# Linear attention's chunk means: the squares of a head's two halves are added on VectorE, and one mean product per chunk stands in place of two

## The chip, the cores and the metric

The kernel is one launch on one core of a Trainium2 chip. The metric is the device time of the launch in microseconds (us); before the change it is 3007.17 us, the median of three runs (3007.15, 3007.17 and 3008.69). Five engines run their own instruction queues side by side and meet only at semaphores: PE (TensorE, matmuls), DVE (VectorE), ACT (ScalarE), POOL (GpSimd) and SP (SyncE, which issues the DMAs).

## The reference

The program is two transformer-like blocks over 512 tokens of width 1024. The change lies in the gated linear attention of the last layer. Its output is normalised per token and head over the 256 values of the head, and then gated:

```python
def _rmsnorm(x, gain):
    xf = x.astype(jnp.float32)
    y = xf * lax.rsqrt(jnp.mean(xf * xf, axis=-1, keepdims=True) + RMS_EPS)
    return (y * gain.astype(jnp.float32)).astype(x.dtype)

# in _gla_mixer: 4 heads (GLA_HEADS) of 256 values (GLA_HV)
    _, o = lax.scan(step, state0, (qc, kc, vc, gc))
    o = o.transpose(1, 0, 3, 2, 4).reshape(bsz, seq, GLA_HEADS, GLA_HV).astype(h.dtype)
    gate = jax.nn.silu(g_out).reshape(bsz, seq, GLA_HEADS, GLA_HV)
    o = _rmsnorm(o, norm_gain) * gate
    return o.reshape(bsz, seq, GLA_VAL_DIM) @ w_out
```

The mean of squares over a head's 256 values is what is computed in another way after the change.

## The kernel before

Activations lie transposed: features on the 128 partitions, tokens along the free dimension. A head's 256 values are therefore two halves of 128 partitions. The recurrence goes over the 512 tokens in four chunks of 128 (`NCH = 4`, `CH = 128`). All order is written out by hand, each engine's queue as a Python function, with counting semaphores between them.

PE's queue for chunk c is: `local(c)` (the part inside the chunk, 8 matmuls of 128 columns, L1528), `chunk_mean(c - 1)` (L1537), `carry(c)` (what the state gains, 4 matmuls of 256 columns, L1544), `across(c)` (the part from the state, L1553, which signals `lo_done`). After chunk 3 come the output products: `glo_half(o, half)` multiplies 256 tokens of the normalised result with output tile o in 24 matmuls of 256 columns (L893, L894, L895). Their order is `glo_half(2, 0)`, `chunk_mean(3)`, `glo_half(3, 0)`, then `glo_half(0, 0)` and `glo_half(1, 0)`, then the second halves of tokens.

`chunk_mean(c)` multiplies a 128x128 matrix that holds 1/256 with the squares. There are 8 square slices of 128 tokens per chunk (4 heads, 2 halves). Two matmuls of 512 columns go into one PSUM bank: the first with all first halves, the second with all second halves, accumulated.

ACT's queue for chunk c: squares of 128x1024 into `lsq` (L2070, signals `lo_sq`), a copy of the raw result into `loT` (L2071, signals `lo_copied`), and the square root of the mean (L2077, signals `lo_std`). Between them stand `high_piece(0)` and `high_piece(1)` (L1609), the high parts of the finished chunks 0 and 1. `high_piece(1)` stands in front of the root of chunk 2.

POOL multiplies each copied chunk by the gate in place (L883, 128x1024, signals `lo_gated`).

DVE's queue: `state_step(c)` (L2764, 4 instructions, PSUM and SBUF), `inverse(c)` (L2787, a reciprocal of 128x512), `scaled(c)` (L2774, the product with the inverse root) and `low_piece(i)` (L2781, the low parts). `glo_half(o, 0)` needs `low_piece(0)` and `low_piece(1)`; the second halves of tokens need the later pieces one after the other. Of the pieces, 0 is chunk 0, 1 is chunk 1, 2 and 3 are halves of chunk 2, and 4 to 7 quarters of chunk 3.

Of the kernel before, what the change touches and what calls it, by code (L numbers as in the profile page):

```python
# [32 lines left out]
ALU = mybir.AluOpType  # L33
# [3 lines left out]
T = 512  # L37
# [36 lines left out]
CH = P  # L74
# [89 lines left out]
M_ID, M_D, M_256, M_128, M_64, M_ROT = range(6)  # L164
# [102 lines left out]
def program(nc, a, out, gates):  # L267

    with ExitStack() as ctx:
        sems = {}  # L270

        def S(name):
            if name not in sems:
                sems[name] = ctx.enter_context(nc.semaphore(name))
            return sems[name]
# [33 lines left out]
        pb = ctx.enter_context(nc.psum_tensor("pb", [P, 8, 512], F32))  # L309
# [17 lines left out]
        def mat(n):  # L327
            return mats[:, n, :]
# [164 lines left out]
        at_lev = G.at  # L493
# [12 lines left out]
        la = Area(at_lev + 4 * T).take(4, T)  # L506
        loT = Area(at_lev + 8 * T).take(DC, T)
        lsq = Area(at_lev + 6 * T).take(DC, CH)
        lkt = Area(at_gw).take(TT, GH, P)

        pieces = [(0, 0, 8), (1, 0, 8), (2, 0, 4), (2, 4, 8), (3, 0, 2), (3, 2, 4), (3, 4, 6), (3, 6, 8)]
# [376 lines left out]
        def _(pe):  # L888
            mm = pe.matmul
# [59 lines left out]
            for c in range(DC):  # L949
# [3 lines left out]
                if c == 4:  # L953
                    slot(T_QKD)
                pe.wait_ge(S("h_done"), c + 1)
                m = three(pb[:, QK_BANK[0], :], rhigh[:, w, c, :], rlow[:, w, c, :], hS[:, 0, c, :], hS[:, 1, c, :],
                          c == 0, c == DC - 1)
# [176 lines left out]
            for o in range(DC):  # L1134
# [7 lines left out]
                for c in range(6):  # L1142
                    if o == 0:
                        pe.wait_ge(S("cat_split"), c + 1)
                    m = three(pb[:, b0 + 2 + c // 4, :], rhigh[:, w, c, :], rlow[:, w, c, :], cat_high[:, c, :],
                              cat_low[:, c, :], c % 4 == 0, c in (3, 5))
# [7 lines left out]
            for i in range(PH + 1):  # L1154
# [9 lines left out]
                if i >= 1:  # L1164
# [6 lines left out]
                    for half in range(2):  # L1171
                        for t in range(TT):
                            m = mm(pb[:, 2 + 2 * (s % 2) + half, t * P:(t + 1) * P],  # L1173
                                   qh[:, s % 2, half, t * P:(t + 1) * P], keys[:, half, :],
                                   start=True, stop=True)
# [31 lines left out]
            for n in range(3):  # L1207
                for t in range(TT):
                    src = (choice[:, n, t, :] if n < 2 else
                           score[:, t, :, :].rearrange("p h k -> p (h k)"))  # L1210
                    m = pe.transpose(pb[:, 4 + n, t * P:(t + 1) * P], src, mat(M_ID))
# [60 lines left out]
            for half in range(2):  # L1272
                w = slot(T_PLE + 5 * half)
                for o in range(4):
                    if half:
                        pe.wait_ge(S("x_upd"), X_PEER + o + 1)
                    for c in range(2):
                        m = mm(pb[:, o, :], ring[:, w, o * 2 + c, :], pT[:, c, :], start=c == 0, stop=c == 1)  # L1278
# [192 lines left out]
            for c in range(DC):  # L1471
                m = three(pb[0:16, 4, :], gkwh[:, c, :], gkwl[:, c, :], hS[:, 0, c, :], hS[:, 1, c, :],
                          c == 0, c == DC - 1)
            m.then_inc(S("gk_low"), 1)
            for n in range(4 * TT):
# [4 lines left out]
                if n == 0:  # L1480
                    pe.wait_ge(S("gk_low"), 2)
                    pe.wait_ge(S("l_copied"), 8)
                    for h in range(GH):
                        m = mm(pb[:, h, :], gku[0:16, h * P:(h + 1) * P], gkl[0:16, :], start=True, stop=True)
# [6 lines left out]
            for t in range(TT):  # L1491
                for h in range(GH):
                    m = pe.transpose(pb[:, t, h * P:(h + 1) * P], lks[:, 0, h * T + t * P:h * T + (t + 1) * P],
                                     mat(M_ID))
# [3 lines left out]
            for n in range(NL + 1):  # L1498
# [9 lines left out]
                for t in range(TT):  # L1508
                    for h in range(GH):
# [5 lines left out]
                        m = mm(pb[:, t, h * P:(h + 1) * P], k, q, start=True, stop=True)  # L1515
# [14 lines left out]

            def chunk_mean(c):

                pe.wait_ge(S("lo_sq"), c + 1)
                if c >= 2:
                    pe.wait_ge(S("lo_std"), c - 1)
                for v in range(2):
                    m = mm(pb[:, 4 + c % 2, :].rearrange("p (h i) -> p h i", i=CH), mat(M_256),  # L1537
                           lsq.rearrange("p (h v) i -> p v h i", v=2)[:, v, :, :], start=v == 0, stop=v == 1)
                m.then_inc(S("lo_mean"), 1)

            def carry(c):

# [549 lines left out]
        def _(ve):  # L2092
# [663 lines left out]
            def state_step(c):  # L2756

                ve.wait_ge(S("state_mm"), c + 1)
                ve.wait_ge(S("state_done"), c + 1)
                if c >= 1:  # L2760

                    ve.wait_ge(S("lo_done"), c)
                for h in range(GH):
                    m = ve.scalar_tensor_tensor(state[(c + 1) % 2][:, h, :], state[c % 2][:, h, :], ebl[:, h * NCH + c:h * NCH + c + 1],  # L2764
                                                pb[:, (2 if c else 4) + h // 2, (h % 2) * 256:(h % 2 + 1) * 256],
                                                ALU.mult, ALU.add)
                m.then_inc(S("state_done"), 1)
# [8 lines left out]
            def low_piece(i):  # L2776

                c, n0, n1 = pieces[i]
                at = slice(c * CH, (c + 1) * CH)
                ve.wait_ge(S("h_high"), H_LO + i + 1)  # L2780
                ve.tensor_tensor(hS[:, 1, n0:n1, at], loT[:, n0:n1, at], hS[:, 0, n0:n1, at].bitcast(F32),  # L2781
                                 ALU.subtract).then_inc(S("h_done"), 1)

            def inverse(c):

                ve.wait_ge(S("lo_std"), c + 1)
                ve.reciprocal(rstd[:, c % 2, :], rstd[:, c % 2, :]).then_inc(S("rstd_done"), 1)  # L2787

            def scaled(c):

                ve.wait_ge(S("rstd_done"), 6 + c + 1)
                ve.wait_ge(S("lo_gated"), c + 1)
                for i in range(8):
                    if pieces[i][0] == c:
                        scale_piece(i).then_inc(S("h_raw"), 1)
                ve.sem_inc(S("lo_scaled"), 1)

            state_step(0)
            inverse(0)
            state_step(1)  # L2800
            scaled(0)
            inverse(1)
            state_step(2)
            scaled(1)
            low_piece(0)
            low_piece(1)
            inverse(2)
            scaled(2)
# [119 lines left out]
```

## Time and profile before

| what | value |
|---|---|
| median of three runs | 3007.17 us |
| the profiled execution's own time | 3008.21 us |
| its span, first to last instruction | 3006.4 us |
| PE busy | 2977.3 us, 99% |
| DVE busy | 1694.8 us, 56% |
| ACT busy | 1275.5 us, 42% |
| POOL busy | 1428.6 us, 48% |
| mean granted TensorE clock | 0.997 |

The trace is of one execution. Its own time is 1.8 us above its span and 1.04 us above the median. A timeline row gives the start from the span's beginning, the length, the engine, the line in the kernel, the operation with output and inputs, and in brackets the idle time before it and what ended it. PE's rows overlap, since matmuls are pipelined; the pace of a group is read from one start to the next. An fp32 matmul of the program leaves two matmul records. DVE's and ACT's rows start up to 0.1 us before the instruction in front of them ends. `s_arena` is the SBUF area that holds most intermediate tiles, `lsq`, `loT` and the new `lsum` among them; `pb` is PSUM.

### The profile page before, as it was taken

How to read it: one execution, taken by the hardware profiler on the slowest of the kernel's cores; microseconds unless marked ns; L12 is line 12 of the kernel's file. 1: busy time of each engine (PE TensorE's matmuls, PEld its weight loads, DVE VectorE, ACT ScalarE, POOL GpSimd, SP SyncE). 2: the span in 40 equal slices, each digit the busy share in tenths (PEclk: the TensorE clock that was granted, in tenths of full speed). 3: DMA queues.
4: the chain of work that ended last, by engine and by line, in shares of the span. 5: the costliest groups of instructions: out<-in, count | busy, mean ns of one | idle time of the engine just before them, and what ended most of it. 6: DMA issues, size and time to landing. Idle time of an engine off the chain costs nothing.

```text
span 3006.4 us, 40609 instructions
## 1 busy us (share of the span) xinstructions
PE 2977.3 (99%) x15170; PEld 2561.0 (85%) x15170; DVE 1694.8 (56%) x2918; ACT 1275.5 (42%) x2109; POOL 1428.6 (48%) x747
## 2 busy tenths in 40 slices
PE   9999999999999999999999999999999999999998
PEld 7887888888888888899999997778888889888887
DVE  5826359998999601168888875363122436641223
ACT  6555344325777633333333334354233334542332
POOL 6732444444334444577777603644444433344442
PEclk9999999999999999999999999999999999999999
DMA  4242332444687865599999953212333322123332
GB/s 147 92 139 79 105 101 85 137 146 133 177 214 200 214 192 165 189 341 375 364 368 366 368 188 112 81 61 98 98 95 94 110 70 71 49 92 98 98 98 84
DMA packets 331164, 473.18 MB, mean 157 GB/s; under 512 B 125765, under 2 KB 235237, under 8 KB 330489
## 3 DMA queue, kind: packets, MB, share of 16 engines
q1 hardware_dynamic: 308472, 403.79, 42.4%
q0 software_dynamic: 22528, 67.19, 6.1%
q8 instruction: 106, 1.74, 0.2%
q14 instruction: 58, 0.47, 0.0%
HBM read 405.97 MB, written 60.86 MB: 155 GB/s over the span
## 4 chain that ended last, share of the span: by engine, by line
PE 95%; issue 1%; DVE 1%; POOL 1%; DMA 1%; ACT 0%; SPq 0%; DVEq 0%; POOLq 0%; ACTq 0%
PE pb L893 29%; PE pb L895 29%; PE pb L894 29%; PE pb L1223 2%; PE pb L1515 1%; POOL s_over L753 1%; PE pb L1074 1%; PE pb L1102 0%; PE pb L1173 0%; PE pb L1356 0%; DMA s_ring<-w 0%; PE pb L1376 0%; PE pb L1041 0%; PE pb L1278 0%; PE pb L1365 0%
## 5 line engine op out<-in xcount | busy, mean ns | idle before, releaser
L753 POOL TENSOR_TENSOR s_over<-s_ring,s_rhigh 128x1024 fp32r<-128x1024 f32 x401 | 986.8, 2463 | 1375.3 <-ACT s_rhigh L1623 1374.7
L1623 ACT ACTIVATE s_rhigh<-s_ring 128x1024 fp32r<-128x1024 f32 x525 | 555.8, 1060 | 1098.3 <-DMA s_ring<-w 496.7
L893 PE MATMUL pb<-s_over,s_rhigh 128*128 128x512 f32 (+1 forms) x2392 | 876.5, 366 | 0.5 <-DVE s_over L2470 0.4
L895 PE MATMUL pb<-s_over,s_over 128*128 128x512 f32 (+1 forms) x2392 | 872.8, 365 | 0.0
L894 PE MATMUL pb<-s_over,s_rhigh 128*128 128x512 f32 (+1 forms) x2392 | 872.7, 365 | 0.0
L893 PE MATMUL pb<-s_hS,s_rhigh 128*128 128x512 f32 (+1 forms) x1664 | 650.3, 391 | 5.0 <-DVE s_hS L2781 2.5
L895 PE MATMUL pb<-s_hS,s_over 128*128 128x512 f32 (+1 forms) x1672 | 645.3, 386 | 0.0
L894 PE MATMUL pb<-s_hS,s_rhigh 128*128 128x512 f32 (+1 forms) x1664 | 642.2, 386 | 0.0
L893 PEld LDWEIGHTS pb<-s_over,s_rhigh 128*128 128x128 f32 x2392 | 449.1, 188 | 55.1 <-issue 1.0
L894 PEld LDWEIGHTS pb<-s_over,s_rhigh 128*128 128x128 f32 x2392 | 449.1, 188 | 53.4 <-issue 1.0
L895 PEld LDWEIGHTS pb<-s_over,s_over 128*128 128x128 f32 x2392 | 449.0, 188 | 52.8
L893 PEld LDWEIGHTS pb<-s_hS,s_rhigh 128*128 128x128 f32 x1664 | 313.3, 188 | 71.9 <-issue 6.8
L895 PEld LDWEIGHTS pb<-s_hS,s_over 128*128 128x128 f32 x1672 | 314.0, 188 | 64.8
L894 PEld LDWEIGHTS pb<-s_hS,s_rhigh 128*128 128x128 f32 x1664 | 313.4, 188 | 63.7 <-issue 3.8
L2310 DVE TENSOR_TENSOR s_xT<-pb,s_xT 128x512 f32<-128x512 f32 x95 | 65.5, 690 | 305.2 <-PE pb L895 305.2
L2470 DVE TENSOR_TENSOR s_over<-s_ring,s_rhigh 128x1024 fp32r<-128x1024 f32 x124 | 151.9, 1225 | 93.3 <-ACT s_rhigh L1623 93.0
L2449 DVE TENSOR_SCALAR s_over<-s_arena,s_over 128x128 fp32r<-128x128 f32 x384 | 202.1, 595 | 0.0
L816 POOL DMA_INDIRECT s_arena<-acts,s_arena x128 | 163.2, 1275 | 38.9 <-issue 38.7
L2464 DVE TENSOR_TENSOR s_over<-s_std,s_over 128x384 fp32r<-128x384 f32 x128 | 77.6, 607 | 132.7 <-ACT s_over L1801 132.7
L2659 DVE SCALAR_TENSOR_TENSOR s_arena<-pb,s_rstd 128x512 f32<-128x512 f32 x64 | 44.0, 691 | 178.5 <-PE pb L895 178.4
L2478 DVE TENSOR_TENSOR s_std<-s_arena 128x384 f32<-128x384 f32 x128 | 74.7, 584 | 100.2 <-DMA s_arena<-gates 99.0
L1819 ACT ACTIVATE s_over<-s_over,s_arena 128x128 fp32r<-128x128 f32 x384 | 117.9, 395 | 7.2 <-DVE s_over L2449 6.9
(310 smaller groups left out, 3160.1 us busy)
## 6 DMA issues: line engine op xcount, KB each, us to landing
s_ring<-w SPq DMA_DIRECT2D x272, 512.0 KB, 3.5
s_ring<-eu SPq DMA_DIRECT2D x128, 512.0 KB, 4.0
s_ring<-ev SPq DMA_DIRECT2D x128, 512.0 KB, 6.1
acts<-s_arena SPq DMA_DIRECT2D x128, 256.0 KB, 4.1
s_arena<-acts SPq DMA_DIRECT2D x128, 192.0 KB, 5.1
s_arena<-gates SPq DMA_DIRECT2D x128, 192.0 KB, 6.3
gates<-s_arena SPq DMA_DIRECT2D x36, 512.0 KB, 5.6
gates<-s_arena SPq DMA_DIRECT2D x6, 1024.0 KB, 7.5
```

The source lines that it names most:

```text
L753: gp.tensor_tensor(rlow[:, s, :, :], ring[:, s, :, :], rhigh[:, s, :, :].bitcast(F32), ALU.subtract).then_inc(S("w_split"), 1)
L816: gp.indirect_dma_start(s_act[:, j:j + 1], None, acts1, bass.IndirectOffsetOnAxis(ap=s_el[:, j:j + 1], axis=0))\
L893: mm(dst, a_high, b_high, start=start, stop=False)
L894: mm(dst, a_high, b_low, start=False, stop=False)
L895: return mm(dst, a_low, b_high, start=False, stop=stop)
L1623: sc.activation(rhigh[:, s, :, :], ring[:, s, :, :], ACT.Copy).then_inc(S("w_high"), 1)
L1819: sc.activation(oh1[:, t % 16, 1, :], oh1[:, t % 16, 0, :].bitcast(F32), ACT.Identity, scale=g_ratio[:, t:t + 1]).then_inc(S("oh_low"), 1)
L2310: return ve.tensor_tensor(xT[:, c, :], pb[:, bank, :], xT[:, c, :], ALU.add)\
L2449: ve.tensor_scalar(oh1[:, t % 16, 0, :], iota, chT[:, 0, t:t + 1], g_high[:, t:t + 1].bitcast(F32), ALU.is_equal, ALU.mult).then_inc(S("oh ...
L2464: ve.tensor_tensor(actE[:, k % NA, 1, :], std[:, k % 2, 0:TD], actE[:, k % NA, 0, :].bitcast(F32), ALU.subtract).then_inc(S("e_act"), 1)
L2470: ve.tensor_tensor(rlow[:, n % RING, :, :], ring[:, n % RING, :, :], rhigh[:, n % RING, :, :].bitcast(F32), ALU.subtract).then_inc(S("w_sp ...
L2478: ve.tensor_tensor(std[:, e % 2, 0:TD], va_in[:, e % 4, 0:TD], gtile[:, e % 4, 0:TD], ALU.mult)\
```

## The change

ACT still writes the 8 square slices. A new DVE instruction per chunk, `sum_halves(c)`, adds the second halves to the first into `lsum` (128x512) and signals `lo_sum`. `chunk_mean(c)` is one matmul of 512 columns on `lsum` and waits for `lo_sum` in place of `lo_sq`. `lsum` is a single buffer, so `sum_halves(c)` also waits for the mean of the chunk before.

```diff
+        lsum = Area(at_lev + 5 * T).take(T)
...
             def chunk_mean(c):
 
-                pe.wait_ge(S("lo_sq"), c + 1)
+                pe.wait_ge(S("lo_sum"), c + 1)
                 if c >= 2:
                     pe.wait_ge(S("lo_std"), c - 1)
-                for v in range(2):
-                    m = mm(pb[:, 4 + c % 2, :].rearrange("p (h i) -> p h i", i=CH), mat(M_256),
-                           lsq.rearrange("p (h v) i -> p v h i", v=2)[:, v, :, :], start=v == 0, stop=v == 1)
-                m.then_inc(S("lo_mean"), 1)
+                mm(pb[:, 4 + c % 2, :], mat(M_256), lsum, start=True, stop=True).then_inc(S("lo_mean"), 1)
...
+            def sum_halves(c):
+
+                ve.wait_ge(S("lo_sq"), c + 1)
+                if c >= 1:
+                    ve.wait_ge(S("lo_mean"), c)
+                v = lsq.rearrange("p (h v) i -> p v h i", v=2)
+                ve.tensor_tensor(lsum.rearrange("p (h i) -> p h i", i=CH), v[:, 0, :, :], v[:, 1, :, :], ALU.add)\
+                    .then_inc(S("lo_sum"), 1)
...
             state_step(0)
+            sum_halves(0)
             inverse(0)
             state_step(1)
+            sum_halves(1)
             scaled(0)
             inverse(1)
             state_step(2)
+            sum_halves(2)
             scaled(1)
             low_piece(0)
+            sum_halves(3)
             low_piece(1)
```

On DVE, from `state_step(0)` to `inverse(2)`, the queue stood as follows before (s_std and s_sq hold the state by turns, L2787 is the reciprocal, L2774 `scaled`, L2781 the two `low_piece`):

```order
L2764 SCALAR_TENSOR_TENSOR s_std<-s_sq,s_arena,pb 128x256 x3
L2787 RECIPROCAL s_rstd<-s_rstd 128x512 [waits lo_std]
L2764 SCALAR_TENSOR_TENSOR s_sq<-s_std,s_arena,pb 128x256 [waits lo_done,state_done,state_mm]
L2764 SCALAR_TENSOR_TENSOR s_sq<-s_std,s_arena,pb 128x256 x3
L2774 TENSOR_TENSOR s_arena<-s_arena,s_rstd 128x8x128 [waits lo_gated,rstd_done]
L2787 RECIPROCAL s_rstd<-s_rstd 128x512 [waits lo_std]
L2764 SCALAR_TENSOR_TENSOR s_std<-s_sq,s_arena,pb 128x256 [waits lo_done,state_done,state_mm]
L2764 SCALAR_TENSOR_TENSOR s_std<-s_sq,s_arena,pb 128x256 x3
L2774 TENSOR_TENSOR s_arena<-s_arena,s_rstd 128x8x128 [waits lo_gated,rstd_done]
L2781 TENSOR_TENSOR s_hS<-s_arena,s_hS 128x8x128 [waits h_high] x2
L2787 RECIPROCAL s_rstd<-s_rstd 128x512 [waits lo_std]
```

The same stretch after the change reads so; L2788 is `sum_halves`, and the other lines have moved a little (L2762 for L2764, L2794 for L2787, L2772 for L2774, L2779 for L2781):

```order
L2788 TENSOR_TENSOR s_arena<-s_arena 128x512 [waits lo_sq]
L2794 RECIPROCAL s_rstd<-s_rstd 128x512 [waits lo_std]
L2762 SCALAR_TENSOR_TENSOR s_sq<-s_std,s_arena,pb 128x256 [waits lo_done,state_done,state_mm]
L2762 SCALAR_TENSOR_TENSOR s_sq<-s_std,s_arena,pb 128x256 x3
L2788 TENSOR_TENSOR s_arena<-s_arena 128x512 [waits lo_mean,lo_sq]
L2772 TENSOR_TENSOR s_arena<-s_arena,s_rstd 128x8x128 [waits lo_gated,rstd_done]
L2794 RECIPROCAL s_rstd<-s_rstd 128x512 [waits lo_std]
L2762 SCALAR_TENSOR_TENSOR s_std<-s_sq,s_arena,pb 128x256 [waits lo_done,state_done,state_mm]
L2762 SCALAR_TENSOR_TENSOR s_std<-s_sq,s_arena,pb 128x256 x3
L2788 TENSOR_TENSOR s_arena<-s_arena 128x512 [waits lo_mean,lo_sq]
L2772 TENSOR_TENSOR s_arena<-s_arena,s_rstd 128x8x128 [waits lo_gated,rstd_done]
L2779 TENSOR_TENSOR s_hS<-s_arena,s_hS 128x8x128 [waits h_high]
```

Behind the last of these rows the fourth sum stands between `low_piece(0)` and `low_piece(1)`. The sums of chunks 1 and 2 stand behind a `state_step` and ahead of a `scaled`.

On PE, at the mean of chunk 1 (between `local(2)` and `carry(2)`), the queue was before:

```order
L1528 MATMUL pb<-s_arena 128x128 [waits lo_copied]
L1528 MATMUL pb<-s_arena 128x128 x7
L1537 MATMUL pb<-s_arena,s_mats 128x512 [waits lo_sq]
L1537 MATMUL pb<-s_arena,s_mats 128x512
L1544 MATMUL pb<-s_arena 128x256 [waits state_done]
```

And it is after the change:

```order
L1529 MATMUL pb<-s_arena 128x128 [waits lo_copied]
L1529 MATMUL pb<-s_arena 128x128 x7
L1537 MATMUL pb<-s_arena,s_mats 128x512 [waits lo_sum]
L1542 MATMUL pb<-s_arena 128x256 [waits state_done]
L1542 MATMUL pb<-s_arena 128x256 x3
```

One matmul is gone and the other waits for DVE's sum. Nothing else on PE, and nothing on ACT, POOL or SP, is added, removed or moved.

## Rows read from the trace of the kernel before

**Rows 1.** The page: the span, and each engine's busy time.
```profile
span 3006.4 us, 40609 instructions
PE 2977.3 (99%) x15170; PEld 2561.0 (85%) x15170; DVE 1694.8 (56%) x2918; ACT 1275.5 (42%) x2109; POOL 1428.6 (48%) x747
```

**Rows 2.** Timeline of PE: start, length, engine, line, operands, count, idle before.
```profile
2575.73 1.95 PE L1537 MATMUL pb<-s_arena,s_mats 128*128 128x512 f32 x4
2577.52 1.89 PE L1544 MATMUL pb<-s_arena 128*128 128x256 f32 x8
2579.25 1.95 PE L1553 MATMUL pb<-s_arena,s_std 128*128 128x128 f32 x16
...
2582.82 1.88 PE L1537 MATMUL pb<-s_arena,s_mats 128*128 128x512 f32 x4
2584.54 1.89 PE L1544 MATMUL pb<-s_arena 128*128 128x256 f32 x8
...
2589.83 1.88 PE L1537 MATMUL pb<-s_arena,s_mats 128*128 128x512 f32 x4
2591.55 1.95 PE L1553 MATMUL pb<-s_arena,s_std 128*128 128x128 f32 x16
2596.00 0.36 PE L893 MATMUL pb<-s_hS,s_rhigh 128*128 128x256 f32 x1 [2.50 <-DVE s_hS L2781]
...
2600.14 2.22 PE L1537 MATMUL pb<-s_arena,s_mats 128*128 128x512 f32 x4
```

**Rows 3.** Timeline of DVE, the same columns.
```profile
2578.52 3.35 DVE L2787 RECIPROCAL s_rstd<-s_rstd 128x512 f32<-128x512 f32 x1 [6.85 <-ACT s_rstd L2077]
2581.79 1.56 DVE L2764 SCALAR_TENSOR_TENSOR s_sq<-s_std,s_arena,pb 128x256 f32<-128x256 f32 x4
2583.26 1.22 DVE L2774 TENSOR_TENSOR s_arena<-s_arena,s_rstd 128x1024 f32<-128x1024 f32 x1
2585.46 3.35 DVE L2787 RECIPROCAL s_rstd<-s_rstd 128x512 f32<-128x512 f32 x1 [0.98 <-ACT s_rstd L2077]
...
2590.20 1.22 DVE L2774 TENSOR_TENSOR s_arena<-s_arena,s_rstd 128x1024 f32<-128x1024 f32 x1
2591.34 3.38 DVE L2781 TENSOR_TENSOR s_hS<-s_arena,s_hS 128x1024 fp32r<-128x1024 f32 x1
```

**Rows 4.** The chain that ended last, in order of time: two of its pieces.
```profile
2583.25 3.46 POOL s_arena L883
...
2594.64 1.22 DVE s_hS L2781
```

**Rows 5.** Timeline of ACT.
```profile
2574.58 1.00 ACT L2070 ACTIVATE s_arena<-pb 128x1024 f32<-128x1024 f32 x1
...
2576.51 1.28 ACT L2077 ACT_TABLE_LOAD   x1
2577.80 0.69 ACT L2077 ACTIVATE s_rstd<-pb,s_small 128x512 f32<-128x512 f32 x1
2581.23 1.02 ACT L2070 ACTIVATE s_arena<-pb 128x1024 f32<-128x1024 f32 x1 [2.74 <-PE pb L1553]
2582.15 1.02 ACT L2071 ACTIVATE s_arena<-pb 128x1024 f32<-128x1024 f32 x1
2584.74 0.69 ACT L2077 ACTIVATE s_rstd<-pb,s_small 128x512 f32<-128x512 f32 x1 [1.57 <-PE pb L1537]
```

**Rows 6.** Timeline of POOL.
```profile
2576.63 2.34 POOL L883 TENSOR_TENSOR s_arena<-s_arena 128x1024 f32<-128x1024 f32 x1 [1.96 <-ACT s_arena L2071]
...
2590.26 3.37 POOL L883 TENSOR_TENSOR s_arena<-s_arena 128x1024 f32<-128x1024 f32 x1 [3.56 <-ACT s_arena L2071]
```

**Rows 7.** L2110's instructions (ns min/median/max), then one with POOL's beside it.
```profile
L2110 DVE TENSOR_TENSOR s_rstd<-s_rstd,s_sq x48: 676/681/2907, 393.0 to 2989.4; 128x512 f32<-128x512 f32 x48
2624.38 2.91 DVE L2110 TENSOR_TENSOR s_rstd<-s_rstd,s_sq 128x512 f32<-128x512 f32 x1
2624.34 2.40 POOL L753 TENSOR_TENSOR s_over<-s_ring,s_rhigh 128x1024 fp32r<-128x1024 f32 x1 [0.43 <-ACT s_rhigh L1623]
```

**Rows 8.** One stretch: us, busy of PE, PEld, DVE, ACT, POOL, PEclk, DMA.
```profile
2597.40:2600.80 3.40, 3.40 (x16) 3.07 (x15) 3.01 (x3) 0.00 (x0) 0.70 (x1) 0.50 0.02 5
```

## The prediction, written before the result was known

> **What bounds the kernel now.** I read the page first: PE is busy for 2977.3 us of a span of 3006.4 [rows 1]. So the time is PE's, and a change pays only if it takes work off PE without making PE wait. The page is an average, and the change touches about 30 us, so I went to PE's timeline there. PE is without a gap from the first chunk mean to the end of the recurrence, and then stands idle 2.50 us ahead of the first output product at 2596.00, released by DVE's low parts, L2781 [rows 2]. Behind 2596.00 it has no wait that concerns this change. So the span moves by two things: when the output products start (call it T1, now 2596.00), and what is taken off PE behind T1.
>
> DVE's timeline says what makes T1. `scaled(1)` runs 2590.20 to 2591.42. `low_piece(0)` takes 3.38 us from 2591.34 [rows 3], though its twin `low_piece(1)` takes 1.22 us in the chain of waits, 2594.64 to 2595.86 [rows 4]. Beside the slow one, POOL's gate product runs 2590.26 to 2593.63, 3.37 us, where the first of its kind took 2.34 with DVE idle [rows 6]. So POOL waited for `scaled(1)`, then took its turn, and `low_piece(0)` waited for all of it: 2.2 us. A DVE instruction with two SBUF inputs and a POOL product exclude each other for whole instructions. A second place says so with the width of the new sum: 48 additions of 128x512 take 0.68 us at best and 2.91 at worst, and the 2.91 one starts at 2624.38, 0.04 us behind a POOL product [rows 7]. The ends fit: 2624.34 + 2.40 + 0.55 = 2627.29.
>
> **What the change removes.** One of two mean matmuls in each of four chunks. Two take 2577.52 - 2575.73 = 1.79 us in chunk 0, 2584.54 - 2582.82 = 1.72 in chunk 1, and 2591.55 - 2589.83 = 1.72 in chunk 2 [rows 2]. One is worth 0.86 us, the four 3.4 us. Only the fourth lies behind T1; the other three shorten a stretch that ends in a wait.
>
> **What it adds.** Four DVE additions of 128x512, both inputs in SBUF. The trace has no such addition on these tiles. From below each costs 0.68, the best of the 48, and from above 2.91, one that meets POOL [rows 7]. Which it is follows from the schedule, chunk by chunk. All times are from the span's start.
>
> Chunk 0. The squares end at 2574.58 + 1.00 = 2575.58 [rows 5]; DVE is idle until 2578.52 [rows 3]. The sum ends at 2576.3, the mean starts near 2576.4 in place of 2575.73, and `carry(1)` at 2576.4 + 0.86 = 2577.26 in place of 2577.52: 0.26 gained. The first root does not move, since it waits for a table load until 2577.79 [rows 5]; so neither does the first reciprocal, nor `state_step(1)` behind it, 2581.79 to 2583.35 [rows 3].
>
> Chunk 1. All of PE is 0.26 earlier, so the squares start at 2580.97 (before: 2581.23), the copy ends at 2582.15 + 1.02 - 0.26 = 2582.91 [rows 5], and POOL's second product starts at 2583.25 - 0.26 = 2582.99 [rows 4]. But the sum stands behind `state_step(1)`, whose place the row at 2583.26 now holds [rows 3]. It comes 0.27 us behind POOL, so it is blocked until 2582.99 + 2.34 = 2585.33 and ends at 2585.95. `chunk_mean(1)` starts at 2586.05 in place of 2582.82. After its saving `carry(2)` starts at 2586.91 against 2584.54 [rows 2]: 2.37 late. This is the step that I hold to be decisive.
>
> The next chunk follows. The root of chunk 1 started 2584.74 - 2582.82 = 1.92 behind the mean's start [rows 2, 5]; with one matmul less that is 1.06: 2587.11 to 2587.80. The reciprocal (3.35) ends at 2591.18 and `state_step(2)` (1.56) at 2592.65 [rows 3]. On PE `carry(2)` (1.73) and `across(2)` (its 1.95 from 2579.25 end at 2581.20, just ahead of the squares at 2581.23) make the third squares start at 2586.91 + 1.73 + 1.98 = 2590.62, and the copy end at 2592.57 [rows 2, 5].
>
> Chunk 2. The sum can start at 2592.6 and POOL's third product at 2592.65. That is a tie. If DVE is first, the sum ends at 2593.25, POOL holds until 2595.5, and `scaled(1)` ends at 2596.6. If POOL is first, the sum ends at 2595.6 and `scaled(1)` at 2596.75. Both give `scaled(1)` within 0.2 us, against 2591.42 before.
>
> Chunk 3. The fourth sum stands ahead of `low_piece(1)`, and needs the fourth squares. ACT does them only after `high_piece(1)` (2596.65 to 2597.7, it needs `scaled(1)`), and the root of chunk 2 (to 2598.3). They run 2598.2 to 2599.2. The sum ends at 2599.9, `low_piece(1)` at 2601.1, and T1 is 2601.25. In the other order of chunk 2 the fourth `across` ends later, the squares at 2599.5, and T1 is 2601.5. I take 2601.3.
>
> **The sum.** T1 moves by 2601.3 - 2596.0 = +5.3. Behind T1 the fourth mean loses 0.86, and it never waits, as its sum is done before T1. Behind it nothing new is late: the second halves of tokens hang on the fourth mean by root and reciprocal as before, and PE has the same three half products, 72 matmuls, in between. That makes +4.4.
>
> The clock is the last term. PE's idle 2.50 us were followed by half clock (0.50, 1.2 GHz) from 2597.40 to 2600.80 [rows 8]: 3.4 us in which half the work was done, a loss of 1.7. After the change the pause ahead of T1 is about 5 us, and there is a new one of some 3.3 us ahead of `chunk_mean(1)`. Half clock after the longer pause may partly fall into the pause itself, which gives back up to 1.7. Half clock after the new pause slows `carry(2)` and `across(2)` by up to 1.7, and their lateness only partly reaches T1. I take -0.3 for both, with -1.4 to +1.2 kept for the range: +4.1 in all.
>
> The profiled execution took 3008.21, so its like would take 3012.3. It stands 1.04 above the median; on the median of 3007.17 the forecast is 3011.3.
>
> **A rule weighed.** The rows show a DVE product recorded at 2583.26, with its full speed of 1.22 us, beside a POOL product recorded at 2583.25 that took 3.46 [rows 3, 4]. The Trainium skill (SBUF — State Buffer, section "Who interferes with whom") says that a DVE instruction with two SBUF inputs and a GpSimd instruction that reads SBUF use one locked port pair, that the one issued first keeps it for the whole instruction, and that issue order decides who blocks. The trace agrees that it is a lock and no sharing. By the record starts alone the rule would have POOL block DVE at 2583.25, and the row shows the reverse, so leads under about 0.03 us cannot be read off. By the rule chunk 1 costs the full block (lead 0.27 us) and the sum is +4.1; if the two only slowed each other a little it would be the +2.7 of the second rival.
>
> **The rivals.**
> - The loss turns out larger, by a second lock. `low_piece(1)` follows the fourth sum at 2599.9; POOL's fourth product starts when the copy behind the fourth squares ends, near 2600.2. The margin is 0.3 us. If the sum runs late, because `low_piece(0)` is still busy when the squares end, POOL is waiting when the sum ends, as it was in front of `low_piece(0)` before. It then holds `low_piece(1)` until 2600.2 + 2.34, and T1 is near 2603.8. That is +7.8 - 0.86 = +6.9, 3014.1 us: slower by over 0.2%. For it: the tie of chunk 2 and half clock both shift this meeting. Against: the copy takes 1 us and the sum 0.68, so in the ordinary case DVE wins. It decides where `low_piece(0)` ends later than the fourth squares.
> - The second sum wins the lock or POOL comes later than I think. Then it ends at 2583.95, the mean starts at 2584.05, and `carry(2)` at 2584.92, 0.38 late. The squares of chunk 2 start at 2588.63; POOL's third product runs 2590.65 to 2593.0, the third sum is held by it to 2593.6, `scaled(1)` ends at 2594.75, the fourth squares (behind `high_piece(1)` and the root) at 2597.6, `low_piece(1)` at 2599.45. T1 is 2599.6, +3.6 - 0.86 = +2.7: 3009.9. Against it speaks the lead of 0.27.
> - The sums are covered, as in chunk 0, and T1 stays where DVE and POOL put it before. Then only the fourth mean's 0.86 us is gained: 3006.3. The fourth sum ahead of `low_piece(1)` speaks against it even without any block, since its squares wait behind two ACT instructions. All 3.4 us would be 3003.8, which the wait ahead of T1 excludes for three quarters of it.
> - The change does not do what it says: excluded by the order shown, one matmul less and one addition more per chunk.
>
> **How the numbers follow.** Forecast 0.60, its own range 3009.9 to 3012.5. The second lock 0.17, the second sum first 0.17, covered 0.06. About 0.2% (6 us) is what a measurement of this kernel can tell from no change. Forecast and second sum first lie within it; the second lock lies just beyond, as does a forecast with the worst clock: slower 0.20, within 0.78, faster 0.02. The range reaches from below the third case to the second lock: 3008.8 to 3014.3.
>
> **What would show it.** In the profile after: the second sum near 2583.3 taking 2.6 us beside a POOL product, and PE idle some 3.3 us ahead of the second mean; `low_piece(1)` directly behind the fourth sum near 2601; PE idle some 5 us ahead of the output products; the fourth mean one matmul, without a wait. I would be wrong if the second sum takes 0.7 us, if T1 is earlier than 2599, or if half clock appears more than twice from 2570 on.

## The result, and the profile after

The changed kernel takes 3011.6 us (median of 20 runs, 3008.59 to 3014.44) against 3007.13 us (median of 20, 3004.46 to 3009.44). The ratio is 1.0015, 95% interval 1.0009 to 1.0021: 4.5 us slower, 0.15%. The forecast was 3011.3. The profiled execution of after has a span of 3010.5 us against 3006.4. The experiments ran on other chips. On the first of these (e1 to e4) most executions, those of before included, took about 24 us longer (median of before 3031.53, fastest 3005.06); the traces there show pauses of PE and 20 to 27 us of half clock near 1300 us, far ahead of the change. So ratios and traces are compared there, not medians.

Two lengths are used from here on. L is the time from the first product of `local(0)` to the first output product, R that to the first addition to x_T, the running activations, behind them (DVE, L2310; L2308 after). Before, L is 2596.00 - 2570.19 = 25.81 and R 43.72. PE's timeline of after (start, length, line, count, idle before):

```profile
2570.70 2.05 PE L1529 MATMUL pb<-s_arena 128*128 128x128 f32 x16 [1.02 <-DVE s_arena L2719]
...
2576.97 1.10 PE L1537 MATMUL pb<-s_arena,s_mats 128*128 128x512 f32 x2 [0.65 <-DVE s_arena L2788]
2577.90 1.89 PE L1542 MATMUL pb<-s_arena 128*128 128x256 f32 x8
...
2586.57 1.12 PE L1537 MATMUL pb<-s_arena,s_mats 128*128 128x512 f32 x2 [3.21 <-DVE s_arena L2788]
2587.53 3.21 PE L1542 MATMUL pb<-s_arena 128*128 128x256 f32 x8
2590.54 2.34 PE L1551 MATMUL pb<-s_arena,s_sq 128*128 128x128 f32 x16
...
2594.72 1.12 PE L1537 MATMUL pb<-s_arena,s_mats 128*128 128x512 f32 x2
...
2600.98 0.36 PE L894 MATMUL pb<-s_hS,s_rhigh 128*128 128x256 f32 x1 [3.36 <-DVE s_hS L2779]
...
2605.42 1.02 PE L1537 MATMUL pb<-s_arena,s_mats 128*128 128x512 f32 x2
```

The recurrence begins 0.51 us later than before, for reasons ahead of the change. L is 2600.98 - 2570.70 = 30.28, 4.47 longer. Against the gapless PE of before [rows 2] there are three pauses: 0.65 ahead of the first mean, 3.21 ahead of the second, 3.36 ahead of the output products (2.50 before). `carry(2)` took 1.72 us before and takes 3.01 here.

DVE's timeline of after, from the first state step with a sum behind it:

```profile
2582.30 1.56 DVE L2762 SCALAR_TENSOR_TENSOR s_sq<-s_std,s_arena,pb 128x256 f32<-128x256 f32 x4
2583.78 2.73 DVE L2788 TENSOR_TENSOR s_arena<-s_arena 128x512 f32<-128x512 f32 x1
2586.43 1.21 DVE L2772 TENSOR_TENSOR s_arena<-s_arena,s_rstd 128x1024 f32<-128x1024 f32 x1
2588.45 3.35 DVE L2794 RECIPROCAL s_rstd<-s_rstd 128x512 f32<-128x512 f32 x1 [0.80 <-ACT s_rstd L2075]
...
2593.97 0.69 DVE L2788 TENSOR_TENSOR s_arena<-s_arena 128x512 f32<-128x512 f32 x1 [0.69 <-ACT s_arena L2068]
2594.58 1.22 DVE L2772 TENSOR_TENSOR s_arena<-s_arena,s_rstd 128x1024 f32<-128x1024 f32 x1
2595.71 3.39 DVE L2779 TENSOR_TENSOR s_hS<-s_arena,s_hS 128x1024 fp32r<-128x1024 f32 x1
2599.02 0.68 DVE L2788 TENSOR_TENSOR s_arena<-s_arena 128x512 f32<-128x512 f32 x1
2599.62 1.21 DVE L2779 TENSOR_TENSOR s_hS<-s_arena,s_hS 128x1024 fp32r<-128x1024 f32 x1
```

And POOL's gate products of chunks 1, 2 and 3 in the same execution:

```profile
2583.62 2.34 POOL L884 TENSOR_TENSOR s_arena<-s_arena 128x1024 f32<-128x1024 f32 x1 [4.14 <-ACT s_arena L2069]
2594.93 3.09 POOL L884 TENSOR_TENSOR s_arena<-s_arena 128x1024 f32<-128x1024 f32 x1 [8.96 <-ACT s_arena L2069]
2599.68 3.39 POOL L884 TENSOR_TENSOR s_arena<-s_arena 128x1024 f32<-128x1024 f32 x1 [1.66 <-ACT s_arena L2069]
```

The second sum is recorded at 2583.78, 0.16 behind POOL's start, and takes 2.73 in place of 0.7: the step on which the prediction rested. In the row of before at this place POOL was recorded 0.01 ahead, and `scaled(0)` went first [rows 3, 4]. Here POOL leads by enough. By the Trainium skill (SBUF — State Buffer, "Who interferes with whom") the one that issues first keeps the port pair for its whole instruction, and the trace agrees: POOL's product has its full 2.34, and the sum ends 0.55 behind it. Further down the meeting of before is repeated: `low_piece(0)` takes 3.39. The last meeting is near: `low_piece(1)` at 2599.62, POOL at 2599.68, and DVE goes first.

The clock, in two stretches of after (us, busy of PE, PEld, DVE, ACT, POOL, granted clock, DMA share, GB/s):

```profile
2587.90:2591.30 3.40, 3.40 (x12) 2.80 (x11) 2.85 (x1) 1.46 (x2) 0.00 (x0) 0.51 0.00 0
2601.60:2605.00 3.40, 3.40 (x18) 3.40 (x18) 3.37 (x3) 0.00 (x0) 1.47 (x1) 0.50 0.02 5
```

There are two stretches of half clock (1.2 GHz), one behind each long pause, where before had one [rows 8].

### The profile page after: what moved, and what is told of

It reads as the page before. It is cut to its first block, busy times and chain, and to the rows that moved or that the text cites. A ratio compares the mean times of both kernels' runs of the same rounds, so it can differ in the third digit from the quotient of the medians.

```text
span 3010.5 us, 40600 instructions
## 1 busy us (share of the span) xinstructions
PE 2976.5 (99%) x15162; PEld 2561.4 (85%) x15162; DVE 1693.8 (56%) x2922; ACT 1275.6 (42%) x2109; POOL 1423.8 (47%) x747
## 3 DMA queue, kind: packets, MB, share of 16 engines
q1 hardware_dynamic: 308472, 403.79, 42.3%
## 4 chain that ended last, share of the span: by engine, by line
PE 94%; issue 2%; DVE 1%; ACT 1%; POOL 1%; DMA 1%; SPq 0%; DVEq 0%; POOLq 0%; ACTq 0%
PE pb L894 29%; PE pb L895 29%; PE pb L896 29%; PE pb L1224 2%; PE pb L1516 1%; POOL s_over L754 1%; PE pb L1075 1%; PE pb L1103 0%; PE pb L1174 0%; PE pb L1357 0%; DMA s_ring<-w 0%; PE pb L1377 0%; ACT s_rhigh L1621 0%; PE pb L1042 0%; PE pb L1279 0%
## 5 line engine op out<-in xcount | busy, mean ns | idle before, releaser
L2308 DVE TENSOR_TENSOR s_xT<-pb,s_xT 128x512 f32<-128x512 f32 x95 | 65.5, 690 | 305.2 <-PE pb L896 305.1
```

The lines of the kernel that those rows point to most:

```text
L2308: return ve.tensor_tensor(xT[:, c, :], pb[:, bank, :], xT[:, c, :], ALU.add)\
```

## The experiments

One table first. "Half" is the time of half clock while PE worked inside R, read off the granted clock; the last column but one takes half of it off R.

| kernel | L | R | half | R - half/2 | ratio to before, 95% |
|---|---|---|---|---|---|
| before | 25.81 | 43.72 | 3.4 | 42.0 | |
| after | 30.28 | 47.29 | 6.8 | 43.9 | 1.0015, 1.0009 to 1.0021 |
| e1 second sum free of POOL | 29.00 | 47.11 | 5.8 | 44.2 | 1.0014, 0.9996 to 1.0032 |
| e2 fourth sum behind | 29.68 | 46.69 | 6.8 | 43.3 | 0.9990, 0.9966 to 1.0014 |
| e3 one mean matmul, no sums | 24.98 | 41.99 | 3.4 | 40.3 | 1.0003, 0.9973 to 1.0033 |
| e4 sums unread | 28.70 | 47.09 | 4.6 | 44.8 | 1.0027, 1.0012 to 1.0042 |
| e5 after, first POOL waits | 29.21 | 44.71 | 0 | 44.7 | 1.0014, 1.0005 to 1.0023 |
| e6 before, POOL waits | 23.72 | 40.10 | 0 | 40.1 | 0.9991, 0.9982 to 1.0000 |
| e7 both | 25.35 | 42.25 | 0 | 42.3 | 0.9999, 0.9990 to 1.0008 |
| e8 chunks 0 and 3 only | 25.86 | 41.37 | 0 | 41.4 | 1.0000, 0.9990 to 1.0009 |
| e9 before, pause filled | 25.81 | 42.19 | 0 | 42.2 | 0.9997, 0.9988 to 1.0006 |
| e10 after, pauses filled | 31.07 | 48.07 | 3.4 | 46.4 | 1.0009, 1.0000 to 1.0018 |
| e11 after, POOL out of the way | 27.17 | 45.40 | 6.1 | 42.4 | 1.0004, 0.9994 to 1.0013 |
| e12 best | 23.59 | 39.11 | 0 | 39.1 | 0.9989, 0.9980 to 0.9998 |

Each row's L and R are of one profiled execution, and a stretch of half clock moves R by about 1.5, so the medians and the traces are read side by side. Outside R the profiled executions of before, after and e5 to e12 differ too, by up to 3.9 us (span minus R, 2960.4 in e11 to 2964.3 in e10). The intervals of e1 to e4 are 0.3 to 0.6% wide, and only e4's excludes no change; there the traces decide.

**e1. The second sum freed of POOL.**

```diff
                 gp.wait_ge(S("lo_copied"), c + 1)
+                if c == 1:
+                    gp.wait_ge(S("lo_sum"), 2)
```

> The changed kernel, with one wait more: POOL's gate product of chunk 1 starts only when the second sum is done, so POOL cannot hold the port there. L is the time from the first product of local(0) to the first output product: 25.81 us before (2570.19 to 2596.00), 30.28 after (2570.70 to 2600.98). Theory (the second sum is blocked by POOL): its length falls from 2.73 to 0.69 us, PE's idle time ahead of the second mean from 3.21 to about 1.2 us, no half clock follows it, and L is near 29.4, the figure of the prediction's second rival. Rival (the wait comes from the place in DVE's queue behind state_step(1) alone): the second sum and the idle time stay as they are, L 30.3.

DVE's timeline of e1 and the product of chunk 1 on POOL:

```profile
2607.70 0.68 DVE L2790 TENSOR_TENSOR s_arena<-s_arena 128x512 f32<-128x512 f32 x1
...
2615.07 0.68 DVE L2790 TENSOR_TENSOR s_arena<-s_arena 128x512 f32<-128x512 f32 x1
2615.67 3.37 DVE L2774 TENSOR_TENSOR s_arena<-s_arena,s_rstd 128x1024 f32<-128x1024 f32 x1
```
```profile
2608.53 3.21 POOL L886 TENSOR_TENSOR s_arena<-s_arena 128x1024 f32<-128x1024 f32 x1 [5.12 <-DVE s_arena L2790]
```

The second sum takes 0.68, PE's pause ahead of the second mean falls from 3.21 to 1.16, and L is 29.00: the mechanism is shown. But 2 us of pause gave only 1.3 us of L, and R hardly moved: the lock now catches `scaled(1)` (3.37, the order "DVE first" of the forecast's chunk 2), the pause ahead of the output products grows to 4.91, and half clock follows it.

**e2. The fourth sum behind `low_piece(1)`.** In DVE's queue `sum_halves(3)` and `low_piece(1)` change places.

> The changed kernel with the fourth sum behind low_piece(1) in DVE's queue. After the change the fourth squares were done at 2598.68, ahead of low_piece(0)'s end at 2599.10, so the sum cost only itself. Theory: L falls by 0.6 us to 29.7, and the fourth mean still waits for nothing, since a half output product of 3 to 4 us stands in front of it. Rival (the step as the prediction put it: the fourth sum waits for its squares behind ACT's queue and holds low_piece(1)): L falls by 2 us or more.

L is 29.68. The first theory holds: in this schedule the fourth sum costs its own 0.6 us.

**e3. One of the two mean matmuls, no sums.**

```diff
-                for v in range(2):
-                    m = mm(..., lsq...[:, v, :, :], start=v == 0, stop=v == 1)
+                m = mm(..., lsq...[:, 0, :, :], start=True, stop=True)
```

> The kernel before with only the first of the two mean matmuls of each chunk, and no sums: half of the squares are left out of the means. It is the largest gain that PE's side of the change could bring. Theory (the start of the output products is set by DVE and POOL): L stays at 25.8 within 0.3, only the fourth mean's 0.86 us is gained, about 3006.3 us beside 3007.2. Rival (the recurrence is bound by PE): L falls by 2.6 to 23.2, 3.4 us in all, 3003.8 us.

Neither. L falls by 0.83 to 24.98, and from the start of the output products to the x_T addition it is 17.01 in place of 17.91, both with 3.4 us of half clock: 0.90 more. PE's part of the change is worth 1.7 us at most (R 43.72 - 41.99), twice what the prediction's rival allowed. Of the 2.6 us saved ahead of the output products some 1.75 don't reach them: PE now waits for the state twice (0.42 and 0.79), the rest stands in no wait that the timeline lists, and the pause of 2.50 stays. The lock is still there, at other instructions: `scaled(0)` takes 2.56 and `scaled(1)` 2.18, and both low pieces have their 1.22.

**e4. The sums on DVE, read by nobody.** PE has both mean matmuls again; ACT's new wait stands ahead of the squares of chunk c, from 1 on, and `sum_halves(c)` waits for `lo_sum` in place of `lo_mean`.

```diff
             def chunk_mean(c):
-                pe.wait_ge(S("lo_sum"), c + 1)
-                mm(pb[:, 4 + c % 2, :], mat(M_256), lsum, ...)
+                pe.wait_ge(S("lo_sq"), c + 1)
+                for v in range(2):
+                    m = mm(..., lsq...[:, v, :, :], start=v == 0, stop=v == 1)
...
+                    sc.wait_ge(S("lo_sum"), c)
```

> The kernel before with the four sums at the change's places in DVE's queue, but both mean matmuls kept and PE waiting for the squares as before; nobody reads the sums (the next squares wait until the sum of the last is done). It tells DVE's load from PE's wait. Theory A (the sums' place in DVE's queue and their lock with POOL already delay the chain state_step, scaled, low_piece): L near 28.9, 3 us over before, with hardly any idle time of PE ahead of the second mean. Theory B (the cost is PE waiting for the sums): L within 0.7 us of 25.8.

DVE's timeline of e4, from the second sum on, and POOL's product beside it:

```profile
2605.98 0.68 DVE L2792 TENSOR_TENSOR s_arena<-s_arena 128x512 f32<-128x512 f32 x1
2606.58 3.38 DVE L2776 TENSOR_TENSOR s_arena<-s_arena,s_rstd 128x1024 f32<-128x1024 f32 x1
...
2619.62 0.69 DVE L2792 TENSOR_TENSOR s_arena<-s_arena 128x512 f32<-128x512 f32 x1 [1.48 <-ACT s_arena L2072]
2620.23 1.22 DVE L2783 TENSOR_TENSOR s_hS<-s_arena,s_hS 128x1024 fp32r<-128x1024 f32 x1
```
```profile
2605.96 2.91 POOL L884 TENSOR_TENSOR s_arena<-s_arena 128x1024 f32<-128x1024 f32 x1 [4.26 <-ACT s_arena L2073]
```

L is 28.70, 2.9 over before, with PE never waiting for a sum. So theory A: the sums in DVE's queue make L 2.9 longer by themselves, though `scaled(0)` is blocked here and not the sum, so this need not be the same 2.9 of the 4.47 after the change. The sum, recorded 0.02 behind POOL, goes first; POOL takes its turn behind it, and `scaled(0)` pays 2.2 us. Putting one more instruction between `state_step` and `scaled` hands POOL the port.

**e5. POOL held back, first attempt.**

```diff
+                if c == 1:
+                    gp.wait_ge(S("lo_scaled"), 1)
+                if c == 2:
+                    gp.wait_ge(S("h_done"), H_LO + 2)
```

> The changed kernel, with POOL held back so that its gate products never run beside DVE work on the path: the product of chunk 1 waits until scaled(0) is done, that of chunk 2 until low_piece(1) is done. Nothing else moves. L (first product of local(0) to first output product) was 25.81 us before and 30.28 after; with the second sum alone freed of POOL it was 29.00, with the sums unread and PE waiting for the squares 28.70. Theory (most of the loss is DVE blocked by POOL, now at one instruction and now at another, and the rest is the fourth sum waiting ahead of low_piece(1)): no DVE instruction of 0.7 or 1.2 us takes over 1.3, and L is near 27.3. Rival (the loss is the sums' own 0.7 us each and PE's wait for them): L stays over 29.

L is 29.21, and this run tests less than it was meant to. POOL's product of chunk 1 did not wait:

```profile
2581.56 2.73 DVE L2792 TENSOR_TENSOR s_arena<-s_arena 128x512 f32<-128x512 f32 x1
2584.22 1.21 DVE L2776 TENSOR_TENSOR s_arena<-s_arena,s_rstd 128x1024 f32<-128x1024 f32 x1
```
```profile
2581.41 2.34 POOL L888 TENSOR_TENSOR s_arena<-s_arena 128x1024 f32<-128x1024 f32 x1 [4.13 <-ACT s_arena L2073]
```

`lo_scaled` is raised by a count instruction of its own behind the products. POOL had passed its wait by 2581.41, while `scaled(0)` began at 2584.22. That this separate instruction ran ahead is the reading that e11 supports, where the product's own count holds POOL back; it was not measured by itself. The second wait worked.

**e11. POOL held back on the product's own count.** `h_raw` is raised by the products of `scaled` themselves.

```diff
+                if c == 1:
+                    gp.wait_ge(S("h_raw"), raw(H_LO) + 1)
+                if c == 2:
+                    gp.wait_ge(S("h_done"), H_LO + 2)
```

> The changed kernel with POOL's product of chunk 1 held back until scaled(0) has really finished, and that of chunk 2 until low_piece(1) has. In the run of this kind before, the first of these waits was passed 2.8 us ahead of scaled(0), because it hung on a count that DVE's queue raises before the product is done; here it hangs on the product's own count. Theory (POOL's lock and the fourth sum's place make the whole lateness): the second sum takes 0.7, PE's pause ahead of the second mean is 1.2, L is near 27.2. Rival: L stays over 29.

DVE's timeline of e11, around the fourth sum:

```profile
2590.08 1.22 DVE L2783 TENSOR_TENSOR s_hS<-s_arena,s_hS 128x1024 fp32r<-128x1024 f32 x1
2593.08 0.69 DVE L2792 TENSOR_TENSOR s_arena<-s_arena 128x512 f32<-128x512 f32 x1 [1.78 <-ACT s_arena L2072]
2593.69 1.22 DVE L2783 TENSOR_TENSOR s_hS<-s_arena,s_hS 128x1024 fp32r<-128x1024 f32 x1
```

L is 27.17 as expected; no DVE instruction up to `low_piece(1)` is blocked. The fourth sum stands and waits 1.78 us for its squares, with `low_piece(1)` behind it: by these rows its place costs 1.78 + 0.6 = 2.4 us here (no run moved it with POOL out of the way and nothing else), and only 0.6 in e2, where POOL held `low_piece(0)` over the same time. Two causes in parallel hide each other.

**e6. The POOL waits without the change.** The kernel before, with the edit of e5.

> The kernel before, both mean matmuls and no sums, with the same two waits on POOL. Theory (the 3.38 us of low_piece(0) was POOL's lock and set the start of the output products): low_piece(0) takes 1.2, L falls by 2.1 to 23.7, PE's pause ahead of the output products from 2.50 to about 0.4 us, and no half clock follows it, which gives up to 1.7 more: 2 to 4 us faster than before. Rival (something else starts the output products, or POOL's late products delay the second halves of the tokens): L within 0.5 of 25.8, or the gain is lost behind the start.

DVE's timeline of e6 (both low pieces in one row), and the first output product:

```profile
2588.52 1.22 DVE L2778 TENSOR_TENSOR s_arena<-s_arena,s_rstd 128x1024 f32<-128x1024 f32 x1
2589.65 2.43 DVE L2785 TENSOR_TENSOR s_hS<-s_arena,s_hS 128x1024 fp32r<-128x1024 f32 x2
```
```profile
2592.23 0.36 PE L897 MATMUL pb<-s_hS,s_rhigh 128*128 128x256 f32 x1 [0.41 <-DVE s_hS L2785]
```

L is 23.72 and the pause 0.41, as expected. The gain is 2.7 us (3003.23 against 3005.96), with an interval from 0.9982 to 1.0000 that just reaches no change. The first wait was passed early here too, as in e5; it did no harm, since `scaled(0)` keeps its 1.22. So what set the start of the output products before was POOL's lock on `low_piece(0)`. With POOL out of the way on both sides the change costs 27.17 - 23.72 = 3.45 us of L; with POOL in the way on both, 4.47. So about 1.0 of the 4.47 goes with the lock; it is the smaller part.

**e7. Both, and the sums moved.** The changed kernel with the edit of e5, `sum_halves(1)` and `(2)` ahead of their `state_step`, the fourth behind `low_piece(1)`.

> The changed kernel with the same two waits on POOL, the sums of chunks 1 and 2 ahead of their state_step, and the fourth behind low_piece(1). Theory: the second mean waits for nothing, L is near 24.0 (the state_steps are 0.7 later each), and the fourth mean saves its 0.86 behind the start; so about as fast as the kernel before with the POOL waits alone, within 1 us, and 2 to 4 us faster than before. Rival (the sums cost on this path wherever they stand): L over 26.

L is 25.35 and not 24.0; R is 2.15 over e6. PE waits five times in L, 0.63, 0.44, 0.38, 0.43 and 1.53 us, and 1.01 behind it. This run is not clean, as POOL still blocks two instructions: its product of chunk 1, again not held back, makes `scaled(0)` take 2.21 in place of 1.22, and its product of chunk 2, released by `low_piece(1)`, makes the fourth sum take 2.83, ahead of the 1.01 pause behind L. With all of that 1.0 taken off, L would be near 24.4, by estimate, still 0.6 over e6 with two middle mean matmuls fewer; what the middle sums alone cost was not measured.

**e8. Chunks 0 and 3 alone.** `chunk_mean` waits for the sum and uses one matmul for c in (0, 3), and for the squares with two matmuls otherwise; the fourth sum stands behind `low_piece(1)`.

> The change made for chunks 0 and 3 alone, with the fourth sum behind low_piece(1); chunks 1 and 2 keep two mean matmuls and PE waits for the squares there; POOL as before. Theory: the first sum is covered and the fourth stands beside the first half output product, so L is that of the kernel before, 25.6 to 25.8, and from the start of the output products to the first x_T addition (L2310, 17.91 us before) 0.9 us less: 0.9 to 1.1 us faster. Rival: the fourth sum meets POOL's last product and the fourth mean waits for it, which takes the gain back.

L is 25.86, but by another way: `carry(1)` comes 0.15 earlier, POOL's product of chunk 1 is now recorded 0.15 ahead of `scaled(0)` (2583.60 against 2583.75), and `scaled(0)` takes 3.27, `scaled(1)` 2.37, while the low pieces have their 1.22. From the first output product to the x_T addition it takes 15.51 at full clock, where e6 and e9 take 16.38: 0.87 saved. The time shows no gain (ratio 1.0000, interval 0.9990 to 1.0009); 0.9 us is below what it can show.

**e9 and e10. The pauses filled.** In e9 two matmuls that nobody reads follow `across(3)` of the kernel before; in e10, the changed kernel, three stand there and three ahead of the second mean:

```diff
+            def busy(n):
+                for _ in range(n):
+                    mm(pb[:, 5, :], mat(M_256), lqs[:, 0, 0:T], start=True, stop=True)
...
+            pe.wait_ge(S("lo_std"), 2)
+            busy(2)
             glo_half(2, 0)
```

> The kernel before, with two matmuls of 512 columns whose result nobody reads between across(3) and the first output product, in PE's pause of 2.50 us there (each 0.86 us). R is the time from the first product of local(0) to the first x_T addition, 43.72 us before, and holds 3.41 us of half clock under work. Theory (half clock follows the pause, and costs half of its length): no half clock behind the start of the output products, R near 42.0, L unchanged at 25.8, and 1 to 1.7 us faster than before. Rival (half clock comes from something else, or the pause left over is enough for it): R and the time unchanged.

> The changed kernel with three such matmuls ahead of the second mean (pause of 3.21 us) and three ahead of the first output product (3.36 us). It had 6.83 us of half clock under work, in two stretches, and R 47.29. Theory: none of the two is left, R near 43.9 to 44.5, L near 28.6 to 30.3, and the time 1.5 to 3.4 us under that of the changed kernel, so 1 to 3 us over before. Rival (the loss is waiting alone): R over 46 and the time 4 to 5 us over before.

e9: L stays at 25.81, no half clock, R 42.19 (expected 42.0), 1.53 less than before. The trace is as the theory has it, but it is one execution, and e8 and e5 have no half clock behind pauses of 2.68 and 3.21 either; so that the filled pause took it away is not shown. The time is 0.7 us lower, and the interval holds both no gain and 1.7 us.

e10 is divided. The time is as the theory has it: ratio 1.0009, 2.3 us over before where the changed kernel is 4.5 over. R is 48.07, on the rival's side, and L the longest of all. But the profiled execution is the slowest of its 11 (3014.17 us, median 3008.72). What lies outside R differs by 3.9 us at most between the traces, so the usual execution of e10 probably has a shorter R, and no trace shows it. DVE and POOL of e10:

```profile
2594.30 0.68 DVE L2797 TENSOR_TENSOR s_arena<-s_arena 128x512 f32<-128x512 f32 x1
2594.90 3.37 DVE L2781 TENSOR_TENSOR s_arena<-s_arena,s_rstd 128x1024 f32<-128x1024 f32 x1
2598.19 1.21 DVE L2788 TENSOR_TENSOR s_hS<-s_arena,s_hS 128x1024 fp32r<-128x1024 f32 x1
2600.88 0.69 DVE L2797 TENSOR_TENSOR s_arena<-s_arena 128x512 f32<-128x512 f32 x1 [1.48 <-ACT s_arena L2077]
2601.49 1.22 DVE L2788 TENSOR_TENSOR s_hS<-s_arena,s_hS 128x1024 fp32r<-128x1024 f32 x1
```
```profile
2594.36 2.83 POOL L884 TENSOR_TENSOR s_arena<-s_arena 128x1024 f32<-128x1024 f32 x1 [7.29 <-ACT s_arena L2078]
```

With no half clock inside L this execution has the prediction's schedule line by line: the tie of chunk 2 (sum 2594.30, POOL 2594.36), the sum first, `scaled(1)` blocked, the fourth sum waiting for its squares. L is 2602.86 - 2571.79 = 31.07, against the forecast 2601.3 - 2570.19 = 31.1.

**e12. A version to beat both.** e8 with

```diff
+                if c == 1:
+                    gp.wait_ge(S("h_raw"), raw(H_LO) + 1)
+                if c == 2:
+                    gp.wait_ge(S("lo_sum"), 2)
+                if c == 3:
+                    gp.wait_ge(S("h_raw"), raw(H_LO + 3) + 1)
```

> A version to beat both: the change in chunks 0 and 3 alone, fourth sum behind low_piece(1), and POOL's products of chunks 1 to 3 held back until scaled(0), the fourth sum and scaled(2) are done. Theory: L near 23.7 as with the POOL waits alone, where R was 40.10 without half clock, and the fourth mean saves its 0.86: R near 39.3, 3 to 4 us faster than before. Rival (POOL's products of chunks 2 and 3 come too late for the second halves of the tokens): a pause of PE over 0.5 us in front of them, and a time no better than with the POOL waits alone (0.9991 of before).

L is 23.59 and R 39.11, the least of all; no pause stands ahead of the second halves. The time is 3003.3 against 3006.39, ratio 0.9989, interval 0.9980 to 0.9998: 3.1 us faster than before. Beside the POOL waits alone (0.9991) it can't be told apart by time; by the traces it is 1.0 us shorter.

## Why the prediction was right, point by point

**The block of the second sum** was right: 2.73 us, PE's pause 3.21 (forecast 3.3), and e1 takes it away. What was too strong is "the step that I hold to be decisive". Freeing the sum gives 1.3 us of L back; e4, with PE waiting for no sum at all, is still 2.9 over. The late start of the output products is mostly DVE's queue: an instruction more between `state_step` and `scaled` (e4, where the lock then falls on `scaled(0)`), and the fourth sum ahead of `low_piece(1)` (e11).

**Chunk 0.** Forecast 0.26 gained, measured 0.13: the first mean starts 6.27 behind the first product in place of 5.54 [rows 2], `carry(1)` 7.20 in place of 7.33. The sum ends at 2576.81 and the mean starts at 2576.97, so handing over took 0.16 where 0.1 was forecast, and the one matmul took 0.93 to the next group where 0.86 was.

**Chunks 2 and 3, T1.** Forecast +5.3, measured +4.47, and +5.26 in e10. At full clock the schedule was right in the traced execution of e10, the slowest of its runs, and e1 has the same order in chunk 2. In the profiled execution of after, half clock behind the 3.21 us pause made the third squares late, the sum then met nobody, and the lock fell on `low_piece(0)`. The prediction had half clock there in its range, but not this order of chunk 2: both of its orders block `scaled(1)`. The pause ahead of the output products is 3.36 where some 5 was forecast: PE's work ahead of it ends 26.92 behind the first product of `local(0)` (26.15 in e10, whose fills stand behind that), and T1 comes 0.8 earlier.

**The fourth mean.** Forecast -0.86. The stretch from the first output product to the x_T addition is 17.01 against 17.91, with 3.4 us of half clock in both: -0.90. It never waited.

**The clock.** Forecast -0.3, and this term was mis-sized. Half clock under work inside R is 6.8 us in place of 3.4: 3.4 of it inside L, which slows `carry(2)` (3.01 in place of 1.72), and 3.4 behind the start of the output products, as before. So nothing was given back there. A stretch of 3.4 us was also priced too high at 1.7: behind the start of the output products it costs 17.91 - 16.38 = 1.53 (before against e9), since the output products start 0.12 us apart at full clock and 0.21 at half (before, from 2602.31 and from 2597.58), which is less than a factor of two. By its own steps R moved by 4.47 (forecast 5.3) - 0.90 (forecast -0.86) = +3.57, with nothing more behind T1 for the clock (forecast -0.3), against the forecast's +4.1. The span's +4.1 is this 3.57 and the 0.51 us that lie ahead of the change, so it is partly luck that the median came out 0.3 us from the forecast: T1 was forecast 0.8 too late, the clock term 0.3 too low, and the 0.51 was in no term. Other executions draw the clock differently.

**The rivals.** The second sum did not win the lock in the traced execution of the change, nor in e2, e5 or e10, which have the same order there; it did in e4. The second lock came near: 0.06 us between `low_piece(1)` and POOL's product, where 0.3 was forecast. The covered case did not come. But its price was wrong: the prediction said that the wait ahead of T1 excludes three quarters of the 3.4 us; e3 got 1.7, since an earlier third chunk also lets POOL's product end earlier: its third product ends 21.40 behind the first product of `local(0)`, 23.44 before.

## What to carry to other kernels

A matmul taken off a bound engine by an addition elsewhere can pay only where the addition has cover. Here the traces show 0.87 us saved at the last chunk and 0.13 at the first, too little for the time of e8 to show, and a loss where the addition stood between two instructions of the chain that sets the end. Before adding a two-input VectorE instruction, look for the GpSimd products that start near it: which of the two starts first decides who loses a whole instruction, and holding back a GpSimd product that nobody needs yet (2.7 us here, with no other change, at the edge of what the runs can tell) can be worth more than the change. When a change lengthens a pause of TensorE, count the half clock that may follow it, and expect it to differ from run to run.

## What the runs showed of the hardware that was not expected

- A record's start shows who holds the port only from some hundredths of a us on. With POOL recorded 0.01 ahead (before [rows 3, 4]) or 0.02 ahead (e4, 2605.96 against 2605.98; e6 and e9 too) DVE went first. With POOL 0.04 ahead [rows 7], 0.15 (e5, e10) and 0.16 (after) POOL went first, and the addition took 2.73 to 2.91.
- Half clock did not follow every long pause: before had it behind 2.50 us, after behind 3.21 and 3.36; e8 has a pause of 2.68, e5 pauses of 3.21 and 3.06, and both full clock throughout L and R. What decides was not settled.
- A count raised by an instruction of its own in DVE's queue was passed 2.8 us before the product ahead of it began (e5), as far as POOL's start shows, and 1.2 us before it in e7 (2584.11 against 2585.33). ACT waits for the same count before it writes the root of a later chunk; whether that wait can be passed too early was not tried.
